# Reordering a two-block transformer kernel: join of three rearrangements (deferred norm scaling, split operands in free buffers, moved steps)

## What is computed

```python
def first_block(x, ...):                      # once
    u = rmsnorm(h, norm_mix)
    u_ssm, q, k, v = split(u @ w_in)
    y_ssm = s5_branch(u_ssm, ...)             # scan, gelu, * sigmoid(y @ w_glu + b)
    y_attn = stick_breaking_attention(q, k, v)  # 8 heads, strict causal mask
    g_ssm, g_attn = split(sigmoid(u @ w_gate + b_gate))
    merged = g_ssm * (y_ssm @ w_up_ssm) + g_attn * (y_attn @ w_up_attn)
    h = h + merged @ w_out
    hid = relu(rmsnorm(h, norm_mlp) @ w_ff1)
    h = h + (hid * hid) @ w_ff2
    return rmsnorm(h, norm_final)

def hybrid_layer(x, c_act, ...):              # twice
    shift, scale, gate = split(c_act @ w_ada + b_ada)
    u = x * (1.0 + scale) + shift
    ... = split(u @ w_in)                     # a, b, q_lat, kv_lat, k_rope, gates
    y_a = (silu(layer_norm(conv31(a1 * sigmoid(a2)))) * silu(a_gate)) @ w_a_out
    y_b = (gb * conv3(gc * xb) * silu(b_gate)) @ w_b_out
    y_c = (attention(rms_norm(q_lat) @ w_uq, rms_norm(kv_lat) @ w_ukv, rope) * silu(c_gate)) @ w_c_out
    m = g_a * y_a + g_b * y_b + g_c * y_c
    return layer_norm(ALPHA * x + gate * (m @ w_o))
```

## Time and profile before

| | |
|---|---|
| median of three runs | 1154.83 us |
| the profiled execution | 1156.74 us |
| its span, first to last instruction | 1155.0 us |
| mean granted TensorE clock, share of full | 0.947 |
| PE busy | 1051.6 us, 91% of the span |
| DVE busy | 719.8 us, 62% |
| ACT busy | 539.5 us, 47% |
| POOL busy | 355.1 us, 31% |
| chain that ended last, PE's share | 74% |

### The profile page before, as it was taken

The page is one execution under the profiler, slowest core; times in us unless marked ns, Lnnn a source line. Parts: engine busy times, 40 slices in busy tenths (PEclk is TensorE's granted clock), DMA queues, the critical chain, the costliest instruction groups (busy, mean ns, idle before and its releaser), DMA issues.

```text
span 1155.0 us, 19572 instructions
## 1 busy us (share of the span) xinstructions
PE 1051.6 (91%) x8104; PEld 984.3 (85%) x8104; DVE 719.8 (62%) x1076; ACT 539.5 (47%) x620; POOL 355.1 (31%) x151
## 2 busy tenths in 40 slices
PE   4989999778799999987999989998799999899985
PEld 3977767568699999977999989998689999899984
DVE  4938887536432522335877896656448778977553
ACT  5443554533254444426554644543355546445433
POOL 3087772000178787820136600000001356000000
PEclk8977999899999999998999999999999999899988
DMA  8542443456545565545453455464454543544601
GB/s 256 183 146 74 146 141 127 135 181 205 189 155 183 157 202 189 170 155 186 147 178 116 146 161 167 134 199 163 125 184 147 182 130 133 168 154 147 217 3 37
DMA packets 159497, 179.57 MB, mean 155 GB/s; under 512 B 5041, under 2 KB 141745, under 8 KB 159409
## 3 DMA queue, kind: packets, MB, share of 16 engines
q1 hardware_dynamic: 159024, 177.22, 47.5%
q0 software_dynamic: 384, 1.10, 0.3%
HBM read 177.26 MB, written 1.05 MB: 154 GB/s over the span
## 4 chain that ended last, share of the span: by engine, by line
PE 74%; DVE 11%; issue 6%; ACT 5%; POOL 3%; DMA 1%; SPq 0%; ACTq 0%; DVEq 0%; POOLq 0%
PE pg L1643 22%; PE pg L1644 21%; PE pg L1645 21%; DVE area L1144 2%; DVE w_lo L1135 1%; ACT w_hi L852 1%; PE p_s L1733 1%; PE p_y L1799 1%; ACT area L830 1%; DVE area L1152 1%; PE p_o L1833 1%; PE p_s L1637 1%; DMA raw<-in_w_in 1%; DVE rows L1180 1%; ACT h L830 1%
## 5 line engine op out<-in xcount | busy, mean ns | idle before, releaser
L1643 PE MATMUL pg<-u_hi,w_hi 128*128 128x256 f32 x1664 | 488.7, 294 | 42.7 <-DVE u_lo L1144 38.3
L1644 PE MATMUL pg<-u_lo,w_hi 128*128 128x256 f32 x1664 | 479.8, 288 | 0.0
L1645 PE MATMUL pg<-u_hi,w_lo 128*128 128x256 f32 x1664 | 479.3, 288 | 0.0
L1643 PEld LDWEIGHTS pg<-u_hi,w_hi 128*128 128x128 f32 x1664 | 328.3, 197 | 51.4 <-issue 46.5
L754 POOL TENSOR_TENSOR w_lo<-raw,w_hi 128x2048 fp32r<-128x2048 f32 x58 | 268.2, 4634 | 301.5 <-ACT w_hi L852 301.5
L1644 PEld LDWEIGHTS pg<-u_lo,w_hi 128*128 128x128 f32 x1664 | 328.8, 198 | 0.7
L1645 PEld LDWEIGHTS pg<-u_hi,w_lo 128*128 128x128 f32 x1664 | 328.6, 197 | 0.0
L852 ACT ACTIVATE w_hi<-raw 128x2048 fp32r<-128x2048 f32 (+3 forms) x153 | 274.9, 1803 | 73.8 <-issue 38.6
L1135 DVE TENSOR_TENSOR w_lo<-raw,w_hi 128x2048 fp32r<-128x2048 f32 (+3 forms) x95 | 201.3, 2129 | 82.8 <-ACT w_hi L852 82.6
L858 ACT ACTIVATE area<-pg 128x512 f32<-128x512 f32 (+1 forms) x92 | 54.1, 588 | 170.3 <-PE pg L1645 158.5
L1643 PE MATMUL pg<-vb_hi,w_hi 128*128 128x256 f32 x320 | 93.8, 293 | 12.9 <-DVE area L1162 6.9
(11 more groups left out here) (203 smaller groups left out, 1326.6 us busy)
## 6 DMA issues: line engine op xcount, KB each, us to landing
raw<-in_w_in SPq DMA_DIRECT2D x68, 1024.0 KB, 5.2
raw<-in_w_ff SPq DMA_DIRECT2D x32, 1024.0 KB, 5.6
raw<-in_w_ada SPq DMA_DIRECT2D x24, 1024.0 KB, 5.2
raw<-in_w_gate SPq DMA_DIRECT2D x8, 1024.0 KB, 7.7
raw<-in_w_o SPq DMA_DIRECT2D x8, 1024.0 KB, 5.3
raw<-in_w_out SPq DMA_DIRECT2D x4, 1024.0 KB, 6.6
raw<-in_w_b_out SPq DMA_DIRECT2D x4, 1024.0 KB, 5.0
raw<-in_w_c_out SPq DMA_DIRECT2D x4, 1024.0 KB, 5.1
```

Of the source, the lines that this page charges most:

```text
L1643: pe.matmul(dst, w_h, x_h, start=first, stop=False)
L1644: pe.matmul(dst, w_h, x_l, start=False, stop=False)
L1645: return pe.matmul(dst, w_l, x_h, start=False, stop=last_)
```

## The change

It joins three rearrangements, none of which changes what is computed but for rounding.

- **Stick attention and S5 loop.** The first `gate` panel goes ahead of the loop, the others are moved back by one turn; `s5_out`, `s5_y`, `ada` panels are moved; the loop ends after `m` = 7 with `ada` panels 9 and 10. The mask is added to the scores once, on DVE, into SBUF (`stick_z`, two buffers), so `stick_fails` no longer computes the scores a second time into `p_c`, `stick_soft` has one instruction instead of two, and the exponentials are done in place in PSUM; `stick_weights` gets a Relu more on ACT. The gelu is done once over all four tiles after the loop instead of tile by tile in it. A table of S5 is waited for by half. `gate` panel 2 goes from POOL to DVE.
- **Deferred scaling.** `u2` is `h`*gain, split at once, without the root; ReLU of `ff1` is multiplied by the reciprocal root as it leaves PSUM. At the third norm and at the end of layer 0, DVE only multiplies `h` by the reciprocal root; the gain goes into the scale and into `rest_g`, ACT writes `tmp` with scale and shift and then `u_hi`, DVE subtracts. `prescale(0)` is then eight instructions instead of one.
- **Free buffers and moved steps.** `m` is split in four parts into `m_hi`/`m_lo` in the room of `va` and `vb`, each part right after its `merge0` panel. The sums of the latent norms come after the first `a2` panel on PE; one `conv_a` part leaves the place before the last gates; the layer norm of branch A is spread over later panels. Where the first panel of an operand waits for it piece by piece, its matmuls go by k-tile over both column halves, instead of all k-tiles of one half first.

The diff, cut to what is spoken of:

```diff
+POOL_LOW = [("gate", n) for n in range(3, 8)] + [(job, n) for job in ("ff1", "ff2") for n in range(2 * DFF // W)]
...
+        step("modulate", key[1])
...
+    panel("gate", 0, 0, "w_gate", 0, 0, KT, 256, 1)
     ada_panel(0)
     step("ada_take", 0)
-    for m in range(HEADS + 1):
+    for m in range(HEADS):
         f = m // 2
         if m:
             step("stick_weights", m - 1)
-        if m < HEADS:
-            step("stick_soft", m)
-            step("state", 2 * m)
-            step("gate_ahead", len(panels))
-            step("stick_fails", m)
+        step("stick_soft", m)
+        if m % 2 and f:
+            step("s5_y", f - 1)
+        step("state", 2 * m)
+        if m + 1 < HEADS:
+            step("gate_ahead", len(panels) + 1)
+        step("stick_fails", m)
         step("ada_turn", m)
         if m + 1 < HEADS:
             step("stick_scores", m + 1)
-        if m < HEADS:
-            step("bu", 2 * m + 1)
+        step("bu", 2 * m + 1)
+        if m:
+            step("s5_out", m - 1)
+        ada_panel(m + 1)
+        step("ada_take", m + 1)
         if 2 * m + 2 < PAIRS:
             step("bu", 2 * m + 2)
-        if m % 2 and f:
-            step("s5_y", f - 1)
-        if m % 2 == 0 and f >= 2:
-            step("s5_gelu", f - 2)
-        if m < HEADS:
-            panel("gate", 0, m, "w_gate", 0, 256 * m, KT, 256, 1)
-        if m:
-            step("s5_out", m - 1)
-        if m == HEADS:
-            step("s5_y", WT - 1)
-            step("s5_inner", WT - 1)
-        if m < HEADS:
-            step("state", 2 * m + 1)
-        if m % 2 and f:
-            step("s5_inner", f - 1)
+        if m + 1 < HEADS:
+            panel("gate", 0, m + 1, "w_gate", 0, 256 * (m + 1), KT, 256, 1)
+        else:
+            step("stick_weights", m)
+            ada_panel(9)
+            step("ada_turn", 8)
+            step("ada_take", 9)
+            ada_panel(10)
+            step("ada_turn", 9)
+            step("ada_take", 10)
+        step("state", 2 * m + 1)
         if m in (2, 4):
             step("table", f + 1)
         if m:
             step("stick_out", m - 1)
-        if m < HEADS:
-            ada_panel(m + 1)
-            step("ada_take", m + 1)
+    step("stick_out", HEADS - 1)
+    step("ada_turn", 10)
+    step("s5_out", HEADS - 1)
+    step("s5_y", WT - 1)
     step("split", "ctx")
-    ada_panel(9)
-    step("ada_take", 9)
-    step("s5_gelu", WT - 1)
+    step("s5_gelu")
+    panel("up_attn", 0, 0, "w_up_attn", 0, 0, WT, 512, 2)
+    step("s5_gelu_end")
     step("split", "y")
-    panel("up_attn", 0, 0, "w_up_attn", 0, 0, WT, 512, 2)
-    step("ada_turn", 9)
-    ada_panel(10)
-    step("ada_take", 10)
     panel("up_attn", 0, 1, "w_up_attn", 0, 512, WT, 512, 2)
-    step("ada_turn", 10)
     half("glu", 0, "w_glu", W)
     ada_panel(11)
+    step("ada_take", 11)
...
+    step("split_ahead", count["split"] + 1)
+    step("u2_piece", 0)
+    ada_panel(14)
+    norm_sums(1, 3)
+    for j in range(1, 4):
+        step("u2_piece", j)
+    step("ada_take", 14)
...
+                    step("ada_turn", 14 + n)
+                    ada_panel(15 + n)
+                    step("ada_take", 15 + n)
+                if (c, n) == (1, 0):
                     step("ada_turn", 16)
                     step("ada_end", 1)
         if c >= 1:
...
+        step("rope_k", l)
+        panel("a2", l, 0, "w_in_2", 0, A2, KT, 256, 1)
+        step("latent_stats", l)
         step("latent_norm", l)
-        step("rope_k", l)
-        wide("a2", l, "w_in_2", A2, W)
+        panel("a2", l, 1, "w_in_2", 0, A2 + 256, KT, 256, 1)
         step("split", ("ql", l))
         step("split", ("kvl", l))
...
-            else:
...
-                step("ln_a_var", l)
-        half("branch2", l, "w_c_out_2", D)
+        for n in range(2):
+            panel("branch2", l, n, "w_c_out_2", 0, 512 * n, WT, 512, 2)
+            step("ln_a_var" if n else "ln_a_squares", l)
...
-            if n == 0:
+            if n == 1:
                 step("ln_a_out", l)
-            if n == 1:
+            if n == 2:
...
+        for n in range(4):
+            panel("merge0", l, n, "w_in_2", 0, CM + 256 * n, KT, 256, 1)
+            if n:
+                step("split_tiles", l, n - 1)
+        step("split_tiles", l, 3)
...
+        m_hi = nc.alloc_sbuf_tensor_at("m_hi", [P, KT, T], F32R, offset=shared)
+        m_lo = nc.alloc_sbuf_tensor_at("m_lo", [P, KT, T], F32R, offset=shared + 4 * KT * T)
...
+            OPERANDS["m", l] = operand(mer, m_hi, m_lo, [(2 * j, 2 * j + 2) for j in range(4)], "merge0",
+                                       groups_of("branch0", l)[-1])
...
+            def split_tiles(l, j):
+
+                o = OPERANDS["m", l]
+                act.wait_ge(sem("groups"), o["after"] + 1)
+                act.wait_ge(sem("gt_used"), over("gt_used", find("merge0", l, j)["gt"]))
+                a, b = o["pieces"][j]
+                fn(o["hi"][:, a:b, :], o["src"][:, a:b, :], ACT.Copy).then_inc(*c.event("hi", ("m", l), j))
+
...
+            def u2_piece(j, _):
+
+                if j == 0:
+                    act.wait_ge(sem("groups"), OPERANDS["u2"]["after"] + 1)
+                for s, v in emptied([groups_of("out")[j]]):
+                    act.wait_ge(s, v)
+                for i in (2 * j, 2 * j + 1):
+                    fn(u_hi[:, i, :], h[:, i, :], ACT.Identity, scale=col("norm_mlp", i)).then_inc(*(c.event("hi", "u2", j) if i % 2 else c.step()))
+
+            def modulate(l, _):
+
+                o = OPERANDS["u", l]
+                act.wait_ge(sem("groups"), o["after"] + 1)
+                act.wait_ge(sem("scale1"), over("scale1", l))
+                for j in range(4):
+                    act.wait_ge(sem("ln_rows"), over("ln_rows", l - 1, j))
+                    for i in (2 * j, 2 * j + 1):
+                        fn(tmp[:, i, :], h[:, i, :], ACT.Identity, bias=shift1[:, i:i + 1],
+                           scale=scale1[:, i:i + 1]).then_inc(*c.step())
...
+            def s5_gelu(_, __):
+                act.wait_ge(sem("y_rows"), over("y_rows", WT - 1))
+                fn(yt, yv, ACT.Square).then_inc(*c.event("y_sq"))
+                act.wait_ge(sem("y_inner"), over("y_inner"))
+                fn(yt, yt, ACT.Sigmoid, scale=2 * math.sqrt(2 / math.pi) * 0.044715).then_inc(*c.event("y_sig"))
...
-                else:
-
-                    act.wait_ge(sem("soft"), over("soft", hd - 1))
-                fn(stick[0], p_z[:, 0:384], ACT.Abs).then_inc(*c.step())
-                fn(stick[0], stick[0], ACT.Exp, scale=-1.0).then_inc(*c.step())
-                fn(stick[0], stick[0], ACT.Ln, bias=1.0).then_inc(*c.event("log1p", hd))
...
+                for j in range(KT):
...
+            def scaled(l):
+
+
                 before = c.last
-                for j in range(KT):
-
+                for j in range(4):
                     dve.wait_ge(*before)
-                    dst = tmp[:, j, :] if k < 2 else h[:, j, :]
-                    ins = dve.scalar_tensor_tensor(out=dst, in0=h[:, j, :], scalar=col(name, j), in1=rstd[:, 0, :],
-                                                   op0=ALU.mult, op1=ALU.mult)
-                    ins.then_inc(*(c.event("h_rows", j) if k == 2 else c.event("rows", key, j // 2) if j % 2 else c.step()))
-                    if k < 2 and j % 2 and j >= 3:
-                        low(key, j // 2 - 1)
-                if k < 2:
-                    low(key, 3)
+                    dve.tensor_tensor(h[:, 2 * j:2 * j + 2, :], h[:, 2 * j:2 * j + 2, :], spread(rstd[:, 0, :], P, 2, T),
+                                      ALU.mult).then_inc(*c.event("ln_rows", l, j))
+                    if j and l < LAYERS - 1:
+                        if j == 1:
+                            low_halves(first_splits(find("q_lat", l + 1, 0)["s"] + 1, ahead))
+                        low(("u", l + 1), j - 1)
+                if l < LAYERS - 1:
+                    low(("u", l + 1), 3)
+
+            def u2_piece(j, _):
+
+                dve.wait_ge(sem("hi"), over("hi", "u2", j))
+                for i in (2 * j, 2 * j + 1):
+                    stt(u_lo[:, i, :], h[:, i, :], col("norm_mlp", i), u_hi[:, i, :].bitcast(F32), ALU.mult,
+                        ALU.subtract).then_inc(*(c.event("lo", "u2", j) if i % 2 else c.step()))
 
...
+            def stick_scores(hd, _):
+                dve.wait_ge(sem("z"), over("z", hd))
+                tt(stick_z[hd % 2], p_z[:, 0:384], neg1[:, :], ALU.add).then_inc(*c.event("masked", hd))
 
             def stick_soft(hd, _):
 
                 dve.wait_ge(sem("log1p"), over("log1p", hd))
-                stt(stick[1], p_z[:, 0:384], 0.0, stick[0], ALU.max, ALU.add).then_inc(*c.step())
-                tt(stick[1], stick[1], mask1[:, :], ALU.mult).then_inc(*c.event("soft", hd))
...
-                    dve.tensor_scalar(tmp[:, f:f + 2, :], both, 0.0, None, ALU.max).then_inc(*c.bank_free(g))
```

(32 more changed lines are left out.)

171 lines of the change are left out of this document (65 added, 106 removed).

## The result

The changed kernel took 1107.86 us (median of four runs, 1104.97 to 1109.84), the kernel before 1157.0 beside it: a ratio of 0.9576, 95% interval 0.9537 to 0.9614. The forecast was 1096, range 1078 to 1120: inside the range, 12 us slower than forecast. The profiled execution has a span of 1106.8 us, 48.2 less than before.

The account below looks back on a forecast made before the run. The prediction took the kernel as PE-bound, with PE busy 1051.6 of 1155.0 us. Its terms summed to 61.4 us off 1156.7, giving 1095.3; the forecast was 1096 with 2.6 us allowed for small waits, range 1078 to 1120.

Parts of the forecast that it names:

- Rival (a): Loop: softmax chain, not PE, sets the 14.52 us turn, and the serial gelu fills the tail; 1110 us, chance 0.19.
- The turn: Loop turn: recomputed scores gone, 1.05 us less, nothing added on PE; 14.52 becomes 13.47 us.
- The head: Start of the loop: two score recomputations less, a `gate` panel under PE idle; turn 2 begins at 115.0 us, not 117.16.
- The last turn: Loop's end: VectorE's list and a wait for ScalarE's high half make 16.7 us (12 to 19), then `s5_out` 3.6.
- The tail: After the last `s5_out`: serial gelu chain and two VectorE low halves; 33.8 us instead of 42.4, gain 8.6 (0 to 12).
- `out`: `out` panels: idle removed by earlier operand splits and a weight asked for earlier; 3.1 us saved (0 to 3.1).
- `ff1`: Start of `ff1`: first matmul no longer waits for the root, second panel waits 3.4 us; 8.9 us saved (5 to 13).
- `merge1`: Branches A and B: moved `conv_a` part delays the third `merge1` low half, PE loses 3.3 us; the wait's net gain is 0.
- Rival (c): More gained: no second `ff1` stall (5.0 us) and no `merge1` stalls (2 x 4.9); 1081 us, chance 0.06.
- Latents, `q_lat`, `w_o`: Savings by layer: latent norms 0.9 and 2.5 us, `q_lat` 4.1 and 2.3, `w_o` 4.8 and 5.9.
- rival (b): Moved steps wait in other engines' queues, so `w_o`, `q_lat` and latent gains fail; 1117 us, chance 0.09.
- Rival (d): Feed-forward: `ff1` ReLU reading `rstd` in SBUF waits for GpSimd, up to 74 us; 1170 us, chance 0.03.

Follow-up runs that it names:

- experiment 7: Changed kernel with the two removed score matmuls per head redone, and the `ff1` ReLU's multiplication left out: turn 0.85 us longer; feed-forward unchanged.
- Experiment 3: Changed kernel with the two S5 input products next to each other on TensorE in each loop turn: span 1107.3 us.
- Experiment 2: Changed kernel with the first `ada` panel put ahead of the first `gate` panel: span 1097.3 us.
- Experiment 1: Changed kernel with the last S5 state computed on VectorE before the last two `ada` panels instead of after them: span 1098.6 us.
- experiment 11: Changed kernel with seven moves, among them the first two parts of `out`'s operand split before the second `up_ssm` panel: span 1100.5 us.
- Experiment 5: Changed kernel with weight panels split one further ahead, so `ff1` panel 1's high half precedes the squares and root on ScalarE: span 1099.9 us.
- Experiment 4: Changed kernel with the low halves of `merge1` panels 2 and 3 made on GpSimd instead of VectorE, both layers: span 1097.4 us.
- experiments 8 and 9: Against the changed kernel: 8, k-tiles of one column half first again, span 1111.9 us; 9, all parts of `m` split late, 4.4 us longer in each layer.

## Why the prediction was right, and where it was off

- **PE-bound, and time only where PE is empty or slow.** Held. Five turns and the feed-forward have PE full; experiment 7 lengthened the turn by 0.85 us with four small matmuls. Rival (a), a loop at its old pace, fell.
- **The turn.** Forecast 13.47, measured 13.82. The term that failed is "Added on PE: nothing". Between the ends of `gate` panels (162.65 to 177.17 before, 147.51 to 161.33 after) the two S5 products take 1.43 us before and 2.11 after: the change took them apart. They use different sets of 32 rows of the array (`bu`) and had overlapped in part. The score matmuls, put at 1.05, cost 0.85 when they are put back (experiment 7). All matmuls into `p_c` together went from 2.31 to 1.07 us, and `s5_out` with the `ada` panel from 2.85 to 2.71; with the products that makes the 0.70 us from 14.52 to 13.82. Experiment 3 shows what side by side is worth at best: 1.03.
- **The head.** Forecast start of turn 2 at 115.0, measured 119.9. The step that failed is "A `gate` panel now lies ahead of the loop, under what was PE idle". The move put `ada` panel 0 behind it, and with it the transfer of `gate` panel 2. I had not followed the `raw` ring. Experiment 2 gave back 4.1 of the 4.9.
- **The last turn.** Forecast 16.7 + 3.6 with a wait for ScalarE's high half; measured 22.0. The mechanism was the right one, the size 1.7 us short. Experiment 1 removed the wait, for 3.6 us by the second `up_ssm` panel.
- **The tail.** 31.1 instead of 33.8. This term was a guess about a serial chain; that it erred by 2.7 us on the other side hid more than half of the head's loss, and is luck.
- **`out`.** Forecast 3.1, measured 0.3. Not seen: `ada` panel 12, now moved, had stood in the serial add, round and subtract of the operand and covered 1.0 us of it. The gap is 3.30 us instead of 1.39 and the panel 10.79 instead of 7.54; the gain of 3.1 at panel 1 made up for it. Early parts shorten the gap: experiment 11. Whether putting back the `ada` panel alone would is not shown, as it was tried only together with them, and the part of the low half ahead of the additions was not tested by itself.
- **`ff1`.** The second panel's wait was forecast with its cause (3.4; measured 3.9). To the end of that panel 7.9 us were saved (forecast 8.9), but the `ada` panels that now lie behind it cost 2.0. Experiment 5 shows the cause.
- **`merge1`.** Forecast "that wait only changes its place", 3.3 us; measured 2.93 and 2.92. Experiment 4 shows that VectorE's list was the cause. Rival (c) put the waits of `ff1` and `merge1` at 14.8 us; experiments 4 and 5 took them away and gained 15.8.
- **Latents, `q_lat`, `w_o`.** Within 1 us each, so rival (b), which had them fail, fell. In `w_o` the forecast named the early parts and the k-order together; experiments 8 and 9 part them.
- **Rival (d)** fell in experiment 7. By the rule of the Trainium skill ("SBUF — State Buffer", the section on the two separate sides) that was to be so, and the traces agree on both sides of it: conv multiply-adds with an operand in PSUM took 11.46 us for 28 with GpSimd at work and 11.47 without, while a subtraction with both operands in SBUF took 2.95 us at 294.72, where its form takes 0.7, and ended 0.5 us after a low half on GpSimd had.
- **Not foreseen as a whole:** what the terms lacked together. I allowed 2.6 us for small new waits; by stage 13 us of the forecast gains were missing, 5.6 of them in the loop and its tail.

## What to carry to other kernels

When a step is moved in an in-order list, follow what shares its buffer and its queue, not its own time: here most of what was lost came from a weight split or a transfer standing ahead of, or freed by, the moved step. Where TensorE waits for an operand split in parts, splitting the parts as soon as they exist was worth more than the order of the matmuls (2.9 and 1.5 us in `w_o`). Give an engine that stands idle in a stage the work that delays the bound one, if the operands do not meet in the same memory port.
